# Seven block products in place of eight in the up projection of the first feed-forward block

## The reference

```python
def conv_ffn(h, w_up, w_dw, b_dw, w_down):
    u = dwconv(h @ w_up, w_dw, b_dw)        # 1024 -> 2 x 2816, three taps along the tokens
    a, b = jnp.split(u, 2, axis=-1)
    return (jax.nn.silu(a) * b) @ w_down    # 2816 -> 1024
...
        h_lat = h_lat + g2 * conv_ffn(b_lat, ffn_w_up[i], ffn_w_dw[i], ffn_b_dw[i], ffn_w_down[i])
...
            h_ctx = h_ctx + cg2 * conv_ffn(b_ctx, ffn_w_up[i], ffn_w_dw[i], ffn_b_dw[i], ffn_w_down[i])
```

## Time and profile before

| what | value |
|---|---|
| time, median of 3 runs | 2439.16 us (2434.4 to 2441.12) |
| profiled execution, span from first to last instruction | 2433.2 us |
| TensorE busy | 2276.1 us, 94% of the span |
| VectorE, ScalarE, GpSimd busy | 1161.3, 987.4, 852.0 us |
| mean granted TensorE clock over the span | 0.966 of full speed |

### The profile page before, as it was taken

How to read it: one execution, slowest core, us unless ns; L and a number is a source line. 1 busy time by engine, 2 the same in 40 slices (tenths; PEclk the granted TensorE clock), 3 DMA queues, 4 the chain that set the end, 5 groups by cost and what they waited for, 6 DMA issues and landing times.

```text
span 2433.2 us, 37255 instructions
## 1 busy us (share of the span) xinstructions
PE 2276.1 (94%) x14435; PEld 1872.0 (77%) x14435; DVE 1161.3 (48%) x2028; ACT 987.4 (41%) x1673; POOL 852.0 (35%) x445
## 2 busy tenths in 40 slices
PE   4999699999999998999989999989988889999998
PEld 4887487888888886767778888877746777778777
DVE  4699723432043335378444223447475536441441
ACT  5665544332133324378454324444353214332341
POOL 1799224222222234300144444433301114443443
PEclk9999798999999998999999999999898989999999
DMA  8888021222122221200123333332200002333332
GB/s 272 257 270 255 20 61 52 61 64 72 56 61 60 74 66 58 69 10 1 43 86 97 101 90 95 106 99 79 83 1 2 2 1 86 88 101 90 88 106 83
DMA packets 337090, 204.59 MB, mean 84 GB/s; under 512 B 5869, under 2 KB 335159, under 8 KB 336951
## 3 DMA queue, kind: packets, MB, share of 16 engines
q1 hardware_dynamic: 331915, 194.02, 26.7%
q10 hardware_dynamic: 5036, 8.66, 1.1%
HBM read 200.47 MB, written 2.19 MB: 83 GB/s over the span
## 4 chain that ended last, share of the span: by engine, by line
PE 60%; issue 20%; POOL 9%; DVE 5%; ACT 3%; DVEq 1%; SPq 1%; DMA 1%; ACTq 1%; POOLq 0%
PE ps L623 17%; PE ps L624 17%; PE ps L625 17%; POOL w_lo L550 6%; POOL pc L1610 2%; DVE ps L1578 1%; PE ps L1981 1%; PE ps L896 1%; DVE m L3209 1%; PE ps L2009 1%; PE ps L3008 1%; ACT w_hi L593 1%; DMA ada_x<-in_ada_w 1%; PE ps L1670 1%; SPq L774 0%
## 5 line engine op out<-in xcount | busy, mean ns | idle before, releaser
L550 POOL TENSOR_TENSOR w_lo<-raw,w_hi 128x1024 fp32r<-128x1024 f32 (+1 forms) x203 | 525.8, 2591 | 1105.4 <-ACT w_hi L593 1089.4
L623 PE MATMUL ps<-x_hi,w_hi 128*128 128x512 f32 (+1 forms) x1896 | 689.7, 364 | 30.3 <-DVE x_lo L1481 12.5
L624 PE MATMUL ps<-x_lo,w_hi 128*128 128x512 f32 (+1 forms) x1896 | 676.1, 357 | 0.0
L625 PE MATMUL ps<-x_hi,w_lo 128*128 128x512 f32 (+1 forms) x1896 | 674.6, 356 | 0.0
L593 ACT ACTIVATE w_hi<-raw 128x1024 fp32r<-128x1024 f32 (+1 forms) x251 | 280.3, 1117 | 520.3 <-PE ps L625 515.1
L623 PEld LDWEIGHTS ps<-x_hi,w_hi 128*128 128x128 f32 x1896 | 364.7, 192 | 98.1 <-issue 22.7
L624 PEld LDWEIGHTS ps<-x_lo,w_hi 128*128 128x128 f32 x1896 | 365.4, 193 | 52.3 <-issue 3.8
L625 PEld LDWEIGHTS ps<-x_hi,w_lo 128*128 128x128 f32 x1896 | 364.6, 192 | 50.2
L1855 DVE SCALAR_TENSOR_TENSOR f_a<-ps,prm,f_a 128x511 f32<-128x511 f32 (+2 forms) x176 | 116.1, 680 | 371.4 <-ACT f_b L1820 360.5
L623 PE MATMUL ps<-g_hi,w_hi 128*128 128x512 f32 (+1 forms) x704 | 257.1, 365 | 2.1 <-POOL w_lo L550 1.4
L624 PE MATMUL ps<-g_lo,w_hi 128*128 128x512 f32 (+1 forms) x704 | 255.8, 363 | 0.0
(11 more groups left out here) (388 smaller groups left out, 2966.0 us busy)
## 6 DMA issues: line engine op xcount, KB each, us to landing
raw<-in_ffn_w_up SPq DMA_DIRECT2D x88, 512.0 KB, 3.8
ada_tail<-in_ada_w SPq DMA_DIRECT2D x22, 1024.0 KB, 7.4
raw<-in_ffn_w_down SPq DMA_DIRECT2D x32, 704.0 KB, 4.6
raw<-in_w_up SPq DMA_DIRECT2D x44, 512.0 KB, 3.8
ada_s<-in_ada_w SPq DMA_DIRECT2D x20, 1024.0 KB, 7.9
raw<-in_conv_w_pw SPq DMA_DIRECT2D x24, 512.0 KB, 6.2
raw<-in_w_down SPq DMA_DIRECT2D x16, 704.0 KB, 4.6
raw<-in_w_in SPq DMA_DIRECT2D x17, 512.0 KB, 4.0
```

What stands on the lines that cost most here:

```text
L550: pool.tensor_tensor(M.w_lo[:, slot, 0:K * P], M.raw[:, slot, 0:K * P], M.w_hi[:, slot, 0:K * P].bitcast(F32), ALU.subtract).then_inc(lo_r ...
L623: pe.matmul(o, wh, hi[:, k, t0:t0 + tn], start=first, stop=False)
L624: pe.matmul(o, wh, lo[:, k, t0:t0 + tn], start=False, stop=False)
L625: return pe.matmul(o, wl, hi[:, k, t0:t0 + tn], start=False, stop=last)
```

## The change

The product of one pair, [W_a W_b] of 1024 x 256 with x of 1024 x 768, is cut into 2 x 2 blocks: the weights into quarters of 512 x 128 (in the names of the code the first figure says which side, 1 for a and 2 for b, and the second which half of k), x into four blocks of 512 x 384. Instead of eight block products, seven are made (a Strassen-Winograd scheme): A11, S1, S2, S4, S3, A12 and A22, each of 4 k tiles, three passes and 384 columns. S1 = A21 + A22, S3 = A11 - A21, S2 = S1 - A11 and S4 = A12 - S2 are sums of weight quarters that POOL makes for each pair. The matching sums of x (T1 to T4) are made once by DVE before the first such pair, and split into high and low parts by ACT and POOL. In PSUM, ACT copies partial results (`z_copy_act`) and DVE adds them (`z_comb_dve`), and two products accumulate onto what another left.

The first two of the 22 tiles (`PLAIN`) are still made as before, in an up stream of 4 chunks. The other 20 pairs come as quarters of 256 KB on SP's queue (`z_load_sp`), in eight rotating places (`PLACE`), with high parts in a ring of four. The hidden width is cut into four parts of 4, 6, 6 and 6 tiles, each followed by its own down stream of 8 chunks with as many k tiles, and all engines get an order for the block that is written out anew.

```diff
-STREAMS = [("pw1", 16, 8), ("pw2", 8, 8)]
-for _h in (0, 1):
-    STREAMS += [(f"up0{_h}", 2 * HALF, 8), (f"down0{_h}", 8, HALF)]
+QUARTER = TOK // 2
+PLAIN = 2
+DOWN0 = {"down0A": (0, 4), "down0B": (4, 6), "down0C": (10, 6), "down01": (16, 6)}
+STREAMS = [("pw1", 16, 8), ("pw2", 8, 8), ("up00", 2 * PLAIN, 8)]
+STREAMS += [(_name, 8, _tiles) for _name, (_first, _tiles) in DOWN0.items()]
...
-        for u, ks in ((0, range(0, HALF - 1)), (1, range(0, 5)), (0, (HALF - 1,)), (1, range(5, HALF))):
+        K = ROWS_OF[name]
+        early = min(5, K - 1)
+        for u, ks in ((0, range(0, K - 1)), (1, range(0, early)), (0, (K - 1,)), (1, range(early, K))):
             if ks[0] == 0:
                 chunk_start(pe, name, 0, u)
+                pe.wait_ge(freed, from_g - PLAIN - 1)
...
+    Z = ("A11", "S1", "S2", "S4", "S3", "A12", "A22")
+    PAIRS0 = FT - PLAIN
...
+    def z_load_sp(sp, n):
+        up = w_src["up00"]
+        before = 7 * (n - 1)
+        j = n + PLAIN
+        freed_by = {"A22": before, "A21": before + 1, "A12": before + 2, "A11": before + 3}
...
+        for x in ("A22", "A21", "A12", "A11"):
+            if n:
+                wait_free(sp, n, freed_by[x])
+                if x == "A21":
+                    sp.wait_ge(z_sum, 4 * n)
+            k0, c = (0, KD // 2)[x[2] == "2"], ((0, FT)[x[1] == "2"] + j) * P
+            sp.dma_start(M.zq[PLACE[n][x]], up[:, k0:k0 + KD // 2, c:c + P]).then_inc(z_load[x, n % 2], 16)
...
+    def z_low_pool(pool, n, i):
+
+        m, x = 7 * n + i, Z[i]
+        pool.wait_ge(z_hi, m + 1)
+        if x in ("A11", "S1"):
+            pool.wait_ge(z_sum, 4 * n + 3)
+        if x in ("S2", "A12"):
+            pool.wait_ge(z_sum, 4 * n + 4)
+        pool.tensor_tensor(M.zl[PLACE[n][x]], M.zq[PLACE[n][x]], M.zh[m % 4].bitcast(F32), ALU.subtract).then_inc(z_lo, 1)
...
+        if which == "S1":
+            if n == 0:
+                pool.wait_ge(tile_done, done(Q0["up00"] + 3))
+            wait_free(pool, n, before + 4)
...
+            pool.tensor_tensor(z["S1"], z["A21"], z["A22"], ALU.add).then_inc(z_sum, 1)
+        if which == "S3":
+            pool.wait_ge(z_load["A11", n % 2], 16 * (n // 2 + 1))
+            pool.tensor_tensor(z["S3"], z["A11"], z["A21"], ALU.subtract).then_inc(z_sum, 1)
+        if which == "S2":
+            wait_free(pool, n, before + 5)
+            pool.wait_ge(z_sum, 4 * n + 1)
+            pool.tensor_tensor(z["S2"], z["S1"], z["A11"], ALU.subtract).then_inc(z_sum, 1)
+        if which == "S4":
...
+            wait_free(pool, n, before + 6)
+            pool.wait_ge(z_sum, 4 * n + 3)
+            pool.wait_ge(z_load["A12", n % 2], 16 * (n // 2 + 1))
+            pool.tensor_tensor(z["S4"], z["A12"], z["S2"], ALU.subtract).then_inc(z_sum, 1)
+
+    def t_sums_dve(dve, k):
...
+        for n, t in enumerate((k, k + h2)):
+            dve.tensor_tensor(M.y4[:, n, :], M.x_hi[:, t, :].bitcast(F32), M.x_lo[:, t, :].bitcast(F32), ALU.add)
+        dve.drain()
...
+        dve.tensor_tensor(t1, b12, b11, ALU.subtract)
+        dve.tensor_tensor(t3, b22, b12, ALU.subtract)
+        dve.drain()
+        dve.tensor_tensor(t2, t3, b11, ALU.add)
+        dve.drain()
+        dve.tensor_tensor(M.t4[:, k, :], b21, t2, ALU.subtract).then_inc(t_sum, 1)
...
+    def z_product(pe, n, i):
+
+        x, j, m = Z[i], n + PLAIN, 7 * n + i
+        pe.wait_ge(z_lo, m + 1)
...
+        for k in range(KD // 2):
+            hi, lo = z_moving(x, k)
+            pe.matmul(o, wh[:, k, :], hi, start=opens and k == 0, stop=False, skip_group_check=True)
+            pe.matmul(o, wh[:, k, :], lo, start=False, stop=False, skip_group_check=True)
+            mm = pe.matmul(o, wl[:, k, :], hi, start=False, stop=k == KD // 2 - 1, skip_group_check=True)
+        mm.then_inc(z_prod, 1)
...
+    def ffn0_pool(pool):
+        low_stream(pool, "up00", 0, 2)
+        rest_pool(pool, "n20")
+        t_low_pool(pool, 0)
+        low_stream(pool, "up00", 2, 3)
+        t_low_pool(pool, 1)
+        low_stream(pool, "up00", 3, 4)
+        t_low_pool(pool, 2)
+        t_low_pool(pool, 3)
+        for x in ("S1", "S3", "S2"):
+            z_sum_pool(pool, 0, x)
+        for i in range(2):
+            z_low_pool(pool, 0, i)
+        z_sum_pool(pool, 0, "S4")
+        n = 0
+        for name, (first, count) in DOWN0.items():
+            low_stream(pool, name, 0, 2)
+            while n + PLAIN < first + count:
+                opens = opens_part(n)
+                more = n + 1 + PLAIN < first + count
+                for i in range(4 if opens else 2, 7):
+                    if i == 5 and more:
+                        z_sum_pool(pool, n + 1, "S1")
+                        z_sum_pool(pool, n + 1, "S3")
+                    z_low_pool(pool, n, i)
+                if more:
+                    z_sum_pool(pool, n + 1, "S2")
+                    z_sum_pool(pool, n + 1, "S4")
+                n += 1
+                if n + PLAIN < first + count:
+                    for i in range(2):
+                        z_low_pool(pool, n, i)
+            low_stream(pool, name, 2, 5)
+            if n < PAIRS0:
+                for x in ("S1", "S3", "S2", "S4"):
+                    z_sum_pool(pool, n, x)
+            low_stream(pool, name, 5, 8)
+            if n < PAIRS0:
+                for i in range(4):
+                    z_low_pool(pool, n, i)
...
+    def ffn0_act(act):
+        t_high_act(act, 0)
+        high(act, "up00", 0, 0)
+        t_high_act(act, 1)
+        high(act, "up00", 0, 1)
+        mid_act(act, 0, 0)
+        mid_act(act, 0, 1)
+        t_high_act(act, 2)
+        t_high_act(act, 3)
...
+    def ffn0_dve(dve):
+        for k in range(3):
+            t_sums_dve(dve, k)
+        taps_dve(dve, 0, 0)
+        t_sums_dve(dve, 3)
+        taps_dve(dve, 0, 1)
+        product_dve(dve, 0)
+        gate_low_dve(dve, 0)
...
```

More of the change, by code:

```diff
@@ L495, in build_in @@
              "w_out": rows(A["w_out_2"][0], 8)}
-    for b in range(3):
+    w_src["up00"] = rows(A["ffn_w_up"][0], 8)
+    for name, (first, count) in DOWN0.items():
+        w_src[name] = rows(A["ffn_w_down"][0][first * P:(first + count) * P, :], count)
+    for b in (1, 2):
         up = A["w_up_2"][0] if b == 2 else A["ffn_w_up"][b]
@@ new lines, in t4_low_dve, with row, first_half, second_half @@
+    def t4_low_dve(dve):
+        dve.wait_ge(t_hi, 5)
+        dve.tensor_tensor(M.x_lo[:, 0:KD // 2, QUARTER:TOK], M.t4, M.x_hi[:, 0:KD // 2, QUARTER:TOK].bitcast(F32),
+                          ALU.subtract).then_inc(t4_lo, 1)
+    def row(j, t, lo=0, hi=TOK):
+        off = P if j >= PLAIN else 0
+        return M.pair(2 * (j % 2) + t, off + lo, off + hi)
+    def first_half(j, t):
+        return row(j, t, 0, QUARTER)
+    def second_half(j, t):
+        return row(j, t, QUARTER, TOK)
+    def z_moving(x, k):
+        h2 = KD // 2
+        if x[0] == "S" and x != "S4":
+            i = ("S1", "S2", "S3").index(x)
+            return M.t_hi[:, k, i, :], M.t_lo[k][:, i, :]
+        t, c = {"A11": (k, 0), "S4": (k + h2, QUARTER), "A12": (k + h2, 0), "A22": (k, QUARTER)}[x]
+        return M.x_hi[:, t, c:c + QUARTER], M.x_lo[:, t, c:c + QUARTER]
@@ new lines, in build_in, with mid_act @@
+    ZERO_TAP0 = SHIFTS[0].index(0)
+    def mid_act(act, j, t):
+        n = j - PLAIN
+        if n < 0:
+            act.wait_ge(tile_done, done(Q0["up00"] + 2 * j + 2))
+        else:
+            act.wait_ge(z_prod, 7 * n + (6, 7)[t])
+            act.wait_ge(z_comb, 2 * n + 1 + t)
+        if t and j:
+            act.wait_ge(prod_ready, done(j))
+        act.activation(M.f_a[:, t, :], row(j, t), ACT.Identity, scale=ffn_cols(0, ZERO_TAP0, t, 0, j),
+                       bias=ffn_cols(0, None, t, 0, j)).then_inc(mid_ready if t else mid_a, 1)
@@ new lines, in silu_act, with gate_high_act, tile0, taps_dve @@
+    def silu_act(act, j):
+        act.wait_ge(taps_a, j + 1)
+        act.activation(row(j, 0), M.f_a[:, 0, :], ACT.Silu).then_inc(silu_ready, 1)
+    def gate_high_act(act, j):
+        act.wait_ge(prod_ready, done(j + 1))
+        act.activation(M.g0_hi[:, tile0(j), :], row(j, 1), ACT.Copy).then_inc(ghi_ready, 1)
+    def tile0(j):
+        return next(j - first for first, count in DOWN0.values() if first <= j < first + count)
+    def taps_dve(dve, j, t):
+        if t:
+            dve.wait_ge(mid_ready, done(j + 1))
+        else:
+            dve.wait_ge(mid_a, j + 1)
+        for n, tap in enumerate(x for x in range(3) if SHIFTS[0][x]):
+            sh = SHIFTS[0][tap]
+            if n:
+                dve.drain()
+            for t0, t1 in ((0, SEQ), (SEQ, TOK)):
+                o0, o1 = (t0 - sh, t1) if sh < 0 else (t0, t1 - sh)
+                o = M.f_a[:, t, o0:o1]
+                ins = dve.scalar_tensor_tensor(out=o, in0=row(j, t, o0 + sh, o1 + sh), scalar=ffn_cols(0, tap, t, 0, j),
+                                               in1=o, op0=ALU.mult, op1=ALU.add)
+        if t:
+            dve.drain().then_inc(taps_ready, 1)
```

(22 more changed lines are left out.)

267 lines of the change are left out of this document (254 added, 13 removed).

## The result

The changed kernel takes 2490.43 us (median of 4 runs, 2485.34 to 2491.74) against 2438.09 (4 runs, 2434.4 to 2441.12) beside it: a ratio of 1.0206, 95% interval 1.0191 to 1.0220, 52.3 us slower. The forecast was 2473, the range 2453 to 2502. The profiled execution took 2491.74 us, 1.84 more than its span.

What follows compares the result with a forecast made beforehand. PE's matmuls were taken to set the pace, PE busy 94% of 2433.2 us. The terms -42.4 + 44.9 + 6.2 + 8.0 + 16.4 + 0.8 = +33.9 us, added to the median 2439.16, gave 2473; range 2453 to 2502.

Steps and rivals of the forecast that it cites:

- rival (b): Pairs: stalls at A12 let the clock fall if they grow to about 2.7 us; +38 us, 2511; chance 0.12.
- the tail: Last down stream: smaller half chunks cover less of the next norm's sums; +0.8 us, between 0 and 4.
- Matmul saved: Twenty pairs: matmul time falls from 16.68 to 14.56 us each, -42.4 us if PE never waits.
- POOL's price and the loop: Inside parts: POOL operations of 1.25 us, in their order, make a pair 17.55 us; 15 pairs cost +44.9 us.
- The start: Before the first block product: DVE's x sums and POOL's operations exclude each other; PE waits 11.0 us, together +16.4 us.
- high bound: At the start: half clock after both gaps, 3 us lost each, +22 us; left out of the forecast.
- The openings: Four down streams: the third chunk waits for high and low parts, 2.0 us uncovered; +8 us over four parts.
- Rival (a): At the start: the sums of x cost little; +19 us, 2458; chance 0.13.
- (c): Pairs: POOL operations take 1.04 us, the loop 16.1 to 16.35 us; 2453; chance 0.06.
- (d): Pairs: POOL keeps ahead and PE runs at 14.56 us; faster, 2428 at full pace; chance 0.05.
- (e): Block products: no matmul time saved; 384 columns as long as 512, product 2.73 us, loop 20 us; chance 0.01.
- low bound: POOL's price: one 512-column row off the line, 1.04 us, an operation that reads one tensor twice.

Runs made afterwards that it cites:

- E2: E1 plus new orders: GpSimd's low parts of the next pair interleaved with its sums, ScalarE's high parts of S3 and A12 ahead of two copies; 2429.74 us.
- E1: Changed kernel with only GpSimd's order altered: low parts of A12 and A22 go ahead of the next pair's S1 and S3; 2468.81 us.
- E4: Changed kernel with the x sums made from high parts alone, leaving out two of VectorE's six operations a row; 2474.45 us.
- E5: Changed kernel with GpSimd's low parts of the x sums made for one sum of three, VectorE's work untouched; 2477.72 us.
- E6: E2 with two instead of five tiles of each down stream's second chunk ahead of the first chunk's last tile; 2425.49 us.
- E9: E1 with an extra GpSimd operation making S1's first 384 columns twice, plus a drain, lengthening the wait before A11; 2517.07 us, one run.
- E3: Changed kernel, same order, weight sums after the first pair made over 128 of 512 columns, their low parts zeros; 2449.21 us.

## Why the prediction came out as it did

Direction, stated range and mechanism held; the size was 18 us short, beyond my own range of 2462 to 2487. That 2490 still lies in the stated range is partly luck: it reached up there for rival (b), whose falls of the clock came, but without the longer wait that (b) named and at under a third of its 38 us. Up to the norm after the block the profile after is 49.0 us behind the one before, against the predicted 33.9. Term by term, on the 16.68 us of a pair before:

| term | predicted | measured |
|---|---|---|
| start | +16.4 | +16.0 |
| pair 0 | +4.1 | +3.8 |
| 15 pairs inside the parts | +13.1 | +24.3 |
| 4 last pairs of a part | -8.5 | -7.7 |
| four openings and the tail | +8.8 | +12.6 |
| sum | +33.9 | +49.0 |

The measured openings and tail are what the other terms leave of the 49.0.

**Matmul saved.** Right. A product takes 2.09 to 2.11 us instead of 2.08, an unhindered pair 14.7 instead of 14.56; that is the 0.8 us in the last pairs. E2 shows the saving come out nearly in full where nothing waits: 14.70 us in 15 pairs, 1.98 of the 2.12 us a pair.

**POOL's price and the loop.** Right in each of its two waits and in their cause, and E1 and E2 show that it is the order that closes the loop. TensorE waits 1.8 and 0.7 us (2.04 and 0.95 predicted), but its products take longer than planned, so that the loop is mis-sized by 0.2 us: 17.75 in place of 17.55, 3 us in 15 pairs.

**The clock.** This is the step that failed. I put rival (b) at a gap of about 2.7 us and reasoned that the forecast waits lie under the one of 2.19 us that had left the clock alone, so the sum has the falls at nothing. That one gap was no bound. Waits of 1.8 us, once a pair, were followed by half clock in 9 of 15 pairs: 274.5 us less 15 x 17.75 is 8.3 us. It came again at two openings: behind the third chunk's wait of 1.9 us the clock was 0.50 from 777 to 779 us in the third part, and from 937 to 940 in the last one (about 2 us without a matmul there), some 1.6 us each. One of these windows (columns as above):

```profile
777.00:778.00 1.00, 1.00 (x4) 0.81 (x3) 0.00 (x0) 0.00 (x0) 0.00 (x0) 0.50 0.79 239
```

With both, 11.5 of the 15 us are this; the prediction named a falling clock as what would make it wrong. What makes the clock fall behind one wait of 1.8 us and not behind the next stays open.

**The start.** Right to half a microsecond in both places (equal starts differ by up to 2.4 us from profile to profile, so the last microsecond is luck), and E4 and E5 show both halves of its cause: less of VectorE's sums or less of GpSimd's low parts bring the first block product forward by 9.5 and 8.3 us. Rival (a) is out. The half clock that I had left to the high bound did come behind both gaps (0.50 from 398 to 400 and from 422 to 431 us), and the start and pair 0 cost no more than predicted.

**The openings.** Right without the clock: the waits of 1.1 and three times 1.9 us before the third chunk are there, and E6 takes those of the parts of six tiles away by changing, against E2, nothing but how much of the second chunk goes first. In the tail the waits for the sums of the next norm come to 2.2 us where one of 1.6 stood, 0.6 of the 0.8 predicted.

**The other rivals.** (c) needed GpSimd operations of 1.04 us: they take 1.29. (d) needed under 0.93 at this order: the order fell, not the price; with another order PE runs at 14.7 on 1.3 us operations. I had argued from the order written in the change and never asked for the best one. My reading of the earlier trace rows was loose too: the longest wait between 340 and 760 us is one of 2.9 us for VectorE, at 365 us, ahead of the block; 2.2 is the longest inside it. (e) is out by the products of 2.1 us.

**The rest.** 52.3 us in the medians less 49.0 leaves 3.3, in code that the change doesn't touch, and no run assigns it (in the profiles the lag of 49.0 is 47.2 us before the mixers and 56.5 behind them). I had also set the span's forecast on the median of before; the profiled execution of before was some 3 us under that median.

## What to carry to other kernels

An engine that is off the bound by its sum can set the pace by the order of its queue: follow the loop from the operation that frees a buffer round to the one that uses it, and ask which operations between them nobody waits for yet; here new orders in two queues gave back 61 us, more than cutting a third of GpSimd's load did. A trick that saves matmuls needs its operands made somewhere, and of the 42 us saved here some 20 went to make the first ones in a place where nothing could cover them, so look at how a stage starts before counting its steady state. Many short waits of the matmul engine cost more than their length if the granted clock falls behind them, and one gap that left it alone does not show that the next will.

## What the runs showed of the hardware

- Waits of TensorE of 1.7 to 2.0 us were followed by a granted clock of 0.50 in 9 of 15 pairs of the changed kernel and in 2 of 15 in E1; in E4 and E5, which keep the order of the pairs, in 6 and 7 of 15 (one wait of 2.6 us in each among them). Waits of 2.9 us were in 12 of 15. The second wait of a pair, of up to 0.75 us before A11, doesn't tell the changed kernel's pairs apart: it is missing in 5 of the 9 with a fall, and there in 5 of the 6 without. A fall cost from 0.6 to 1.3 us in the changed kernel, 1.7 or 2.8 in E9. Equal waits ended both ways, so the length alone doesn't decide.
- A GpSimd operation of 512 columns that reads one tensor twice took 1.04 us (the zero low parts of E3, 76 of them), one that reads two tensors 1.29: the row that I took for my low bound, which stood off the line, reads one tensor twice as well. 128 columns from two tensors took 0.46. The Trainium skill ("GPSIMD Engine Reference", Elementwise — side-by-side cycle accounting) puts two inputs at about 2.6 cycles an element; the slope from 128 to 512 columns, 0.83 us in 384, is 2.15 ns a column and agrees with it at 1.2 GHz, and the rest of some 0.2 us an operation comes on top.
- While GpSimd's low part of 1152 columns ran beside VectorE's sums it was recorded at 3.2 us in place of 2.6: the waiting counts as busy time on both engines, so neither engine's busy share shows the exclusion. The durations of equal operations do.
